# Seven block products for 16 of the 22 contraction tiles of the down product in a decoder trunk's two FFNs

## The chip, the cores and the metric

The kernel runs on one core of a Trainium2 chip. The metric is the device time of one execution in microseconds, the median of several runs.

## The reference

One inference step of a hybrid decoder trunk, for a prompt of 1024 tokens and 8 single tokens of other sequences: 1032 token columns together, width 1024. The part around the change, cut from the reference:

```
x = x + 0.5 * SwiGLU_1(RMSNorm(x))
... one input projection, an RG-LRU and an SSD head group, one output projection ...
x = x + 0.5 * SwiGLU_2(RMSNorm(x))
final RMSNorm

def swiglu(x, w_gate, w_up, w_down):
    return (silu(x @ w_gate) * (x @ w_up)) @ w_down      # (1024 x 2816), (1024 x 2816), (2816 x 1024)
```

All is float32. D_FF is 2816, so the hidden of an FFN has 22 tiles of 128 rows, and the contraction of the down product runs over these 22 tiles.

## The kernel before

Everything is kept transposed: 128 features on the partitions, the 1032 tokens along the free axis. Each float32 operand of TensorE is split into a high and a low part that it can multiply in one pass (type fp32r in the rows), and a product is the sum of three matmuls, high x high, high x low and low x high.

**Gate and up.** Of the 22 pairs of a gate tile and an up tile of an FFN, two are computed plainly. The other 20 are done in 20 groups (`NG`, number q, 0 to 19) by a scheme of seven block products: the outputs of a group are two tiles (two of gate for an even q, two of up for an odd one), cut into 2 x 2 blocks of output tiles by token halves (516 columns, `HT`), the contraction of 8 tiles is cut in two halves of 4, and seven products of blocks and of sums of blocks (p1 to p7, in the order of `ORDER`: p1, p2, p6, p5, p7, p3, p4) replace eight. One product is 4 contraction tiles x 2 pieces of 258 columns x 3 parts = 24 matmuls, a group 168 (L922). Some products accumulate onto others in PSUM, so between two of them another engine must have read or copied the bank: in `group` of TensorE's program (L876) p6 waits for ScalarE's first copy, p7 for the second (`copied`), p3 for the third, which is that of p5, and p4 waits until VectorE has read the bank of p7 (`c22`).

- Weights: SP loads the two raw tiles of a group; VectorE forms four sums of them (`weight_sums`, L1722 to L1728, 128 x 512 each); ScalarE rounds each of the seven operands to its high part (`operand_high`, L1267) and GpSimd forms the low one (`operand`, L693). The ring holds `RING` = 6 operands.
- ScalarE copies p1, p6 and p5 of each group out of PSUM (`part`, L1301) and does the silu of a gate pair in the odd groups (L1334), at the third step of its `group` (L1320). In group 1 of FFN1 it has besides (`extra`) small preparations for later: the table load at L1397 and the operations of `heads` and `lam`.
- VectorE adds the banks to the copies (`corners`, `join`, L1747), reads p4 (`last_corner`, L1767), scales by the norm's factor (`scale`, L1731) and multiplies gate by up (`product`, L1737) into a pair of hidden tiles, which SP stores to DRAM (`store_hidden`, L466).

**Down.** SP loads the hidden tiles back (`load_hidden`, L471), ScalarE rounds them (L1318), VectorE forms the low parts (`hidden_low`, L1779). TensorE multiplies in three blocks of 8, 8 and 6 contraction tiles (`FFN_BLOCKS`); for each block and each of 8 output tiles m, `products` (L805) calls `nine` (L796, L801) for every contraction tile: 3 pieces of 344 columns x 3 parts = 9 matmuls. The weights of such a unit are split by GpSimd (L670, L672) along a plan's list (`make_plan`). VectorE adds 0.5 x the result to x (`residual`, L1820). The last block of FFN2 is done in three pieces of columns for m from 2 on (L1195), so that the final norm can start early; that doesn't change here.

Each engine has its own program in which all waits stand in order; the seam between group 19 and the down product is written out by hand: VectorE's `lows` puts five `hidden_low` among the joins of group 19.

## Time and profile before

| | |
|---|---|
| runs of the kernel before | 2148.04, 2146.0, 2147.6 us; median 2147.6 |
| the profiled execution | 2145.86 us, its span 2144.1 us |
| mean granted clock of TensorE in it | 0.997 of full speed |
| busy share of the span: TensorE, VectorE, ScalarE, GpSimd | 99%, 60%, 36%, 41% |
| chain that ended last, by engine | TensorE 91%, VectorE 4%, ScalarE 2% |
| read from DRAM, written | 149.37 MB, 46.26 MB; 91 GB/s over the span |

The profile is one execution. A span runs from the first to the last instruction that it shows; the execution's own time is 1.8 us more. The chain of waits follows the work that ended last back from the end: where it runs over TensorE's matmuls, nothing else sets the time. A row of the timeline gives the start, the length and the operation, and in brackets the idle time before it with what ended it. A granted clock of 1.00 is TensorE at 2.4 GHz, 0.50 at 1.2 GHz.

### The profile page before, as it was taken

To read this page: it belongs to the slowest core of one execution; us is meant where nothing else is said; L and a number is where in the kernel's file an instruction comes from. 1 tells how busy PE (TensorE), PEld (TensorE's weight loads), DVE (VectorE), ACT (ScalarE), POOL (GpSimd) and SP (SyncE) were. 2 spreads that over 40 slices of the span, in tenths; PEclk is the share of its full clock that TensorE was granted. 3 is DMA by queue.
4 is the path that set the end of the run, shared out by engine and by line. 5 is a ranking of instruction groups with operands and counts; after the bars stand their busy time and mean duration, and the time that the engine had idled before them with its cause. 6 is when DMAs were issued, how large, how long until landed. Compare 5 with 4: busy or idle time off the path is not lost.

```text
span 2144.1 us, 36027 instructions
## 1 busy us (share of the span) xinstructions
PE 2125.4 (99%) x15378; PEld 2094.4 (98%) x15378; DVE 1292.0 (60%) x1157; ACT 782.3 (36%) x1180; POOL 883.9 (41%) x532
## 2 busy tenths in 40 slices
PE   9999999999999999999999999999999999999998
PEld 9999999999999999999999999999999999999998
DVE  7767565562223557878888596786656556542226
ACT  7433333331001224678786540123433333320004
POOL 4544444433433322443444552333544444434440
PEclk9999999999999999999999999999999999999999
DMA  5122121254222422311111422132212212353222
GB/s 170 60 100 73 66 99 68 91 182 145 98 66 84 138 70 89 120 54 50 37 57 62 157 82 90 50 119 72 87 68 92 79 62 97 120 208 99 89 60 80
DMA packets 64752, 197.80 MB, mean 92 GB/s; under 512 B 9416, under 2 KB 18120, under 8 KB 64592
## 3 DMA queue, kind: packets, MB, share of 16 engines
q1 hardware_dynamic: 63440, 194.97, 26.4%
q8 instruction: 122, 2.00, 0.4%
q10 hardware_dynamic: 1152, 0.52, 0.1%
q14 instruction: 38, 0.31, 0.0%
HBM read 149.37 MB, written 46.26 MB: 91 GB/s over the span
## 4 chain that ended last, share of the span: by engine, by line
PE 91%; DVE 4%; ACT 2%; DVEq 1%; issue 1%; POOL 0%; DMA 0%; ACTq 0%; SPq 0%; POOLq 0%
PE banks L801 44%; PE banks L922 36%; PE banks L845 3%; PE banks L1195 2%; DVE h_lo L1779 0%; PE banks L1106 0%; ACT gate_a L1465 0%; PE banks L953 0%; PE banks L960 0%; PE banks L966 0%; PE banks L1084 0%; PE banks L1102 0%; ACT gate_x L1465 0%; PE banks L1076 0%; DVE decay L2083 0%
## 5 line engine op out<-in xcount | busy, mean ns | idle before, releaser
L672 POOL TENSOR_TENSOR w_lo<-w_raw,w_hi 128x1024 fp32r<-128x1024 f32 (+1 forms) x100 | 270.2, 2702 | 170.8 <-DVE xbc L2054 123.2
L670 POOL TENSOR_SCALAR w_hi<-w_raw 128x1024 fp32r<-128x1024 f32 (+1 forms) x91 | 102.1, 1122 | 565.7 <-PE banks L801 510.3
L801 PE MATMUL banks<-h_hi,w_lo 128*128 128x344 f32 x948 | 303.5, 320 | 0.2 <-DVE up L1747 0.2
L801 PE MATMUL banks<-h_lo,w_hi 128*128 128x344 f32 x948 | 302.9, 319 | 0.0
L801 PE MATMUL banks<-h_hi,w_hi 128*128 128x344 f32 x948 | 302.6, 319 | 0.0
L801 PE MATMUL banks<-u_hi,w_lo 128*128 128x344 f32 x864 | 286.2, 331 | 0.4
L801 PE MATMUL banks<-u_hi,w_hi 128*128 128x344 f32 x864 | 276.4, 320 | 0.0
L801 PE MATMUL banks<-u_lo,w_hi 128*128 128x344 f32 x864 | 276.1, 320 | 0.0
L1820 DVE SCALAR_TENSOR_TENSOR x<-banks,x 128x1032 f32<-128x1032 f32 x42 | 51.8, 1233 | 314.8 <-PE banks L801 314.8
L801 PEld LDWEIGHTS banks<-h_hi,w_lo 128*128 128x128 f32 x948 | 178.0, 188 | 0.4 <-DVE up L1747 0.4
L801 PEld LDWEIGHTS banks<-h_hi,w_hi 128*128 128x128 f32 x948 | 178.4, 188 | 0.0
L801 PEld LDWEIGHTS banks<-h_lo,w_hi 128*128 128x128 f32 x948 | 178.2, 188 | 0.0
L801 PEld LDWEIGHTS banks<-u_hi,w_lo 128*128 128x128 f32 x864 | 162.8, 188 | 7.3 <-issue 5.1
L801 PEld LDWEIGHTS banks<-u_hi,w_hi 128*128 128x128 f32 x864 | 162.9, 188 | 5.1 <-issue 4.3
L801 PEld LDWEIGHTS banks<-u_lo,w_hi 128*128 128x128 f32 x864 | 162.9, 189 | 0.0
L922 PE MATMUL banks<-mix_hi,w_lo 128*128 128x258 f32 x864 | 158.1, 282 | 0.0
L922 PE MATMUL banks<-mix_hi,w_hi 128*128 128x258 f32 x864 | 157.9, 282 | 0.0
L922 PE MATMUL banks<-mix_hi,w 128*128 128x258 f32 x832 | 151.7, 283 | 1.7 <-DVE up L1747 1.7
L1747 DVE TENSOR_TENSOR up<-banks,up 128x516 f32<-128x516 f32 x60 | 41.7, 695 | 165.3 <-PE banks L922 162.6
L1318 ACT ACTIVATE h_hi<-stage 128x1032 fp32r<-128x1032 f32 x44 | 45.8, 1065 | 259.7 <-DMA stage<-hidden 226.5
L922 PE MATMUL banks<-x_hi,w 128*128 128x258 f32 x704 | 130.3, 285 | 4.6 <-ACT up L1301 4.6
L922 PEld LDWEIGHTS banks<-mix_hi,w_lo 128*128 128x128 f32 x864 | 134.0, 189 | 0.0
(353 smaller groups left out, 5661.4 us busy)
## 6 DMA issues: line engine op xcount, KB each, us to landing
w_raw<-in_gate_up SPq DMA_DIRECT2D x46, 512.0 KB, 4.4
hidden<-up SPq DMA_DIRECT2D x44, 516.0 KB, 3.6
stage<-hidden SPq DMA_DIRECT2D x44, 516.0 KB, 3.8
raw<-in_gate_up SPq DMA_DIRECT2D x40, 512.0 KB, 4.3
w_raw<-in_w_in SPq DMA_DIRECT2D x36, 512.0 KB, 4.2
w_raw<-in_down SPq DMA_DIRECT2D x32, 512.0 KB, 4.6
x<-in_xt SPq DMA_DIRECT2D x16, 516.0 KB, 6.7
x_kept<-x SPq DMA_DIRECT2D x16, 516.0 KB, 5.1
```

The lines of the kernel that those rows point to most:

```text
L670: pool.tensor_scalar(w_hi[s][:, 0:n], w_raw[s][:, 0:n], 1.0, 0.0, ALU.mult, ALU.add)
L672: pool.tensor_tensor(w_lo[s][:, 0:n], w_raw[s][:, 0:n], w_hi[s][:, 0:n].bitcast(F32), ALU.subtract).then_inc(split, 1)
L801: end = pe.matmul(out[:, c, 0:CH], w[s][:, k * P:(k + 1) * P], x[kx][:, c * CH:(c + 1) * CH], start=(first and n == 0), stop=(last and n = ...
L845: end = pe.matmul(at[:, c, :], w[s][:, k * P:(k + 1) * P], x, start=(k == 0 and n == 0), stop=(k == KT - 1 and n == 2))
L922: end = pe.matmul(out[:, c, :], w[:, part, k * P:(k + 1) * P], x[:, cols], start=(opens and k == 0 and i == 0), stop=(k == 3 and i == 2), ...
L1195: end = pe.matmul(piece_bank(m, here), w[m][:, k * P:(k + 1) * P], x[FFN_BLOCKS[LAST][0] + k][:, here], start=(k == 0 and n == 0), stop=(k ...
L1318: act.activation(f.hh[j][:], f.stage[n][:], ACT.Copy).then_inc(f.hid_hi.sem, 1)
L1747: dve.tensor_tensor(halved(tile), bank, halved(tile), ALU.add).then_inc(f.ev.sem, 1)
L1820: dve.scalar_tensor_tensor(tile, whole(name), 0.5, tile, ALU.mult, ALU.add).then_inc(set_free[s], 1)
```

## The change

Sixteen of the 22 contraction tiles of each down product go through the seven-product scheme too, as 8 further groups (number q, 20 to 27; `NGT` = 28): two blocks of 8 contraction tiles, and in each four groups, one for each pair of output tiles ("side"). Here the weights of the pair take the place of the gate's, and the hidden takes the place of the normed x. Six contraction tiles (`PLAIN`: 0, 1, 18 to 21) stay as they were, 9 matmuls of 344 columns each. The rows of w_down are put in the order of `DOWN_ORDER` ahead of the launch.

- Tokens' side: VectorE forms four sums and differences of each of 8 hidden pairs (`hidden_mixes`, 128 x 516 each, in the even groups 2 to 16 behind the join of p7); SP stores them to DRAM. A block needs seven operands of the hidden ("slots", 128 x 4 x 516, one for each product, shared by its four groups): SP loads them (`load_slot`, rows of 2064 bytes), ScalarE rounds them (`slot_high`), VectorE forms the low parts (`slot_low`). There are 8 slot buffers for 14 slots in an FFN.
- Down groups: 168 matmuls each like the others; VectorE adds 0.5 x each bank straight into two output tiles of x (`down_group`, seven operations of 516 columns), and p6, p7, p3 and p4 wait for its read of p1, p6, p5 and p7.
- ScalarE: in the groups of gate and up the silu, and `extra` with it, now stands one step later, behind the copy of p5.
- VectorE: the seam of group 19 now holds `slot_low` 0 to 2 and the weight sums of group 20, and group 20 `slot_low` 4 to 6.
- PSUM, the plan of units, norms and stores follow suit; the x of the residual is read from other tiles (`x_again`) than before.

```diff
-FFN_BLOCKS = [(0, 8), (8, 8), (16, 6)]
-LAST = len(FFN_BLOCKS) - 1
+BLOCKS, SIDES = 2, 4
+PLAIN = [0, 1, 18, 19, 20, 21]
+N_LAST = len(PLAIN)
+DOWN_ORDER = [2 * (1 + 4 * b + k) + n for b in range(BLOCKS) for n in range(2) for k in range(4)] + PLAIN
...
+ND = BLOCKS * SIDES
+NGT = NG + ND
+NOPS = 7 * NGT
 RING = 6
+SLOTS = 8
+MIXED = 4 * BLOCKS
...
-        for b, (first, n) in enumerate(FFN_BLOCKS):
-            for m in range(KT):
-                p.unit(("d" + tag, b, m), down[m, :, first * P:(first + n) * P], n)
+        for m in range(KT):
+            p.unit(("d" + tag, m), down[m, :, 8 * BLOCKS * P:], N_LAST)
...
+            def down_weights(f, src, q):
+                b, side = divmod(q - NG, SIDES)
+                group_weights(f, q, [src[2 * side + n, :, 8 * b * P:8 * (b + 1) * P] for n in range(2)])
...
+                if 1 <= i <= MIXED:
+                    sp.wait_ge(*f.h_mixed.past(i))
+                    sp.dma_start(d.hidden_mix[:, i - 1], f.part).then_inc(f.mix_stored.sem, 16)
...
+            def load_slot(f, o):
+                b, n = divmod(o, 7)
+                if o == 0:
+                    sp.wait_ge(used, U(("u" + f.tag, 1)) + 1)
+                elif o < SLOTS:
+                    sp.wait_ge(*f.done.past(7 * (NG - 1) + o))
+                else:
+                    sp.wait_ge(*f.done.past(7 * (NG + SIDES - 1) + o - SLOTS + 1))
+                sp.wait_ge(*f.h_stored.past(32 * (4 * (b + 1) + 1)))
+                sp.wait_ge(*f.mix_stored.past(16 * 4 * (b + 1)))
+                two = d.hidden.rearrange("p (i n) t -> p n i t", n=2)
+                here = slice(1 + 4 * b, 5 + 4 * b)
+                mixed = d.hidden_mix[:, 4 * b:4 * b + 4]
+                src = {"p1": two[:, 0, here, 0:HT], "p2": two[:, 1, here, 0:HT], "p6": mixed[:, :, 1, :], "p5": mixed[:, :, 0, :],
+                       "p7": mixed[:, :, 2, :], "p3": two[:, 1, here, HT:T], "p4": mixed[:, :, 3, :]}[ORDER[n]]
+                sp.dma_start(f.slot_raw[o % SLOTS], src).then_inc(f.slot_landed[o % SLOTS].sem, 16)
...
+            def down(f, x_src, src):
+                load_slot(f, 0)
+                for m in range(2):
+                    x_again(f, x_src, m)
+                down_weights(f, src, NG)
+                for m in range(2, 4):
+                    x_again(f, x_src, m)
+                down_weights(f, src, NG + 1)
+                for o in range(1, SLOTS):
+                    load_slot(f, o)
+                down_weights(f, src, NG + 2)
+                store_hidden(f, NG // 2)
+                sp.wait_ge(*f.h_stored.past(32 * (NG // 2 + 1)))
+                for m in range(4, KT):
+                    x_again(f, x_src, m)
+                    down_weights(f, src, q)
+                for o in range(SLOTS, 7 * BLOCKS):
+                    load_slot(f, o)
+                    down_weights(f, src, q)
...
+                    if q >= NG and (q - NG) % SIDES == 0:
+                        pe.wait_ge(*f.slot_split.past(7 * b + n + 1))
...
+                    if q >= NG and name in ("p6", "p7", "p3", "p4"):
+                        pe.wait_ge(*f.ev.past(read_number(q, {"p6": "p1", "p7": "p6", "p3": "p5", "p4": "p7"}[name])))
...
+            def slot_high(f, o):
+                if o == 0:
+                    act.wait_ge(*f.mix_stored.past(16 * MIXED))
+                act.wait_ge(*f.slot_landed[o % SLOTS].past(16 * (o // SLOTS + 1)))
+                act.activation(f.slot_hi[o % SLOTS], f.slot_raw[o % SLOTS], ACT.Copy).then_inc(f.slot_high.sem, 1)
...
+            first_slot, next_slot = 7 * (NG - 1) + 3, 7 * (NG + SIDES - 1) + 3
+            slots_after = {first_slot + n: n for n in range(SLOTS)}
+            slots_after.update({next_slot + o - SLOTS: o for o in range(SLOTS, 7 * BLOCKS)})
 
             def group(f, q, extra=None):
                 for n in range(7):
-                    if n in (0, 2, 3):
+                    o = 7 * q + n
+                    if q < NG and n in (0, 2, 3):
                         part(f, q, ORDER[n])
-                    if 7 * q + n + RING < NOPS:
-                        operand_high(f, 7 * q + n + RING)
-                    if n == 2:
+                    ahead = {7 * NG - RING + n: () for n in (0, 1)}
+                    ahead.update({7 * NG - RING + 2 + n: (7 * NG + n,) for n in range(4)})
+                    ahead[7 * NG - 1] = (7 * NG + 3, 7 * NG + 4, 7 * NG + 5)
+                    if n == 3 and q < NG:
                         if q == 0:
                             first_silu(f)
                         if extra:
...
                             for tile in f.g[(q // 2 + 1) % 2]:
                                 end = act.activation(tile[:], tile[:], ACT.Silu)
                             end.then_inc(f.silu.sem, 1)
+                    for to in ahead.get(o, (o + RING,)):
+                        if to < NOPS:
+                            operand_high(f, to)
+                    if o in slots_after:
+                        slot_high(f, slots_after[o])
...
+            def hidden_mixes(f, i):
+                if i > 1:
+                    dve.wait_ge(*f.mix_stored.past(16 * (i - 1)))
+                b11, b12, b21, b22 = f.u[0][:, 0:HT], f.u[0][:, HT:T], f.u[1][:, 0:HT], f.u[1][:, HT:T]
+                to = [f.part[:, n, :] for n in range(4)]
+                dve.drain()
+                dve.tensor_tensor(to[0], b11, b12, ALU.subtract)
+                dve.tensor_tensor(to[2], b22, b12, ALU.subtract)
+                dve.drain()
+                dve.tensor_tensor(to[1], b22, to[0], ALU.add)
+                dve.drain()
+                dve.tensor_tensor(to[3], b21, to[1], ALU.subtract).then_inc(f.h_mixed.sem, 1)
...
+            def slot_low(f, o):
+                n = o % SLOTS
+                dve.wait_ge(*f.slot_high.past(o + 1))
+                dve.tensor_tensor(f.slot_lo[n], f.slot_raw[n], f.slot_hi[n].bitcast(F32), ALU.subtract).then_inc(f.slot_split.sem, 1)
...
+            def down_group(f, q, between):
+                side = (q - NG) % SIDES
+                even, odd = f.again[2 * side], f.again[2 * side + 1]
+                left, right = slice(0, HT), slice(HT, T)
+                main, second, third = main_bank(q), twos[1], twos[2]
+                if q < NG + SIDES:
+                    for m in (2 * side, 2 * side + 1):
+                        dve.wait_ge(x_landed[m], 32 if f.tag == "1" else 64)
+                for name, bank, x, part in (("p1", main, even, left), ("p2", second, even, left), ("p6", main, even, right),
+                                            ("p5", third, odd, right), ("p7", main, odd, right), ("p3", third, even, right),
+                                            ("p4", main, odd, left)):
+                    dve.wait_ge(*f.done.past(number(q, name) + 1))
+                    dve.drain()
+                    dve.scalar_tensor_tensor(halved(x[:, part]), bank, 0.5, halved(x[:, part]), ALU.mult,
+                                             ALU.add).then_inc(f.ev.sem, 1)
+                    if between.get(name):
+                        between[name]()
...
+                        between = {"p2": lambda: slot_low(f, 0), "p6": lambda: weight_sums(f, NG), "p7": lambda: slot_low(f, 1),
+                                   "p3": lambda: slot_low(f, 2)}
...
+                hooks = {NG: {"p1": lambda: slot_low(f, 4), "p2": lambda: slot_low(f, 5), "p6": lambda: slot_low(f, 6),
+                              "p5": last_pair, "p7": lambda: product(f, NG // 2, 0),
+                              "p3": lambda: (product(f, NG // 2, 1), weight_sums(f, NG + 1))},
+                         NG + 1: {"p7": lambda: slot_low(f, 7)},
+                         NG + SIDES - 1: {"p7": lambda: slot_low(f, 8), "p3": lambda: slot_low(f, 9),
+                                          "p4": lambda: slot_low(f, 10)},
+                         NG + SIDES: {"p1": lambda: slot_low(f, 11), "p6": lambda: slot_low(f, 12), "p5": lambda: slot_low(f, 13),
+                                      "p3": lambda: weight_sums(f, NG + SIDES + 1)},
+                         NGT - 1: {"p3": lambda: hidden_low(f, 0)}}
```

ScalarE in groups 0 and 1 of FFN1. The first row is the copy of p6 of group 1, `up_1<-banks` that of p5. Before:

```order
L1301 ACTIVATE up_0_82<-banks 128x516
L1267 ACTIVATE w_lo<-raw_0_84 128x512
L1397 ACT_TABLE_LOAD
L1397 ACTIVATE heads<-heads 128x16
L1399 ACTIVATE lam<-lam 128x8
L1334 ACT_TABLE_LOAD
L1334 ACTIVATE gate_2_80<-gate_2_80 128x1032
L1334 ACTIVATE gate_3_81<-gate_3_81 128x1032
L1301 ACTIVATE up_1_83<-banks 128x516
```

and with the change:

```order
L1371 ACTIVATE up_0_82<-banks 128x516
L1335 ACTIVATE w_lo<-raw_0_84 128x512
L1371 ACTIVATE up_1_83<-banks 128x516
L1471 ACT_TABLE_LOAD
L1471 ACTIVATE heads<-heads 128x16
L1473 ACTIVATE lam<-lam 128x8
L1403 ACT_TABLE_LOAD
L1403 ACTIVATE gate_2_80<-gate_2_80 128x1032
L1403 ACTIVATE gate_3_81<-gate_3_81 128x1032
```

The copy of p5 has moved ahead of both table loads, `heads`, `lam` and the silu of the first gate pair.

VectorE in group 19 of FFN1, from the join of p2 on. `up_0<-banks` (L1747) are the joins of p2 and p3, `up_1<-banks` with itself the join of p7, the one with `rstd` the read of p4. Before:

```order
L1747 TENSOR_TENSOR up_0_82<-banks,up_0_82 128x516
L1779 TENSOR_TENSOR h_lo_119<-stage_0_91,h_hi_97 128x1032
L1779 TENSOR_TENSOR h_lo_120<-stage_1_92,h_hi_98 128x1032
L1779 TENSOR_TENSOR h_lo_121<-stage_2_93,h_hi_99 128x1032
L1747 TENSOR_TENSOR up_1_83<-banks,up_1_83 128x516
L1779 TENSOR_TENSOR h_lo_122<-stage_3_94,h_hi_100 128x1032
L1747 TENSOR_TENSOR up_0_82<-banks,up_0_82 128x516
L1779 TENSOR_TENSOR h_lo_123<-stage_4_95,h_hi_101 128x1032
```

and with the change, where L1886 are the reads of group 20:

```order
L1821 TENSOR_TENSOR up_0_82<-banks,up_0_82 128x516
L1867 TENSOR_TENSOR slot_lo_107<-slot_raw_115,slot_hi_99 128x4x516
L1796 TENSOR_TENSOR w_sum_1_89<-raw_0_84,raw_1_85 128x512
L1798 SCALAR_TENSOR_TENSOR raw_1_85<-raw_1_85 128x512
L1800 SCALAR_TENSOR_TENSOR w_sum_0_88<-raw_1_85,raw_0_84 128x512
L1802 TENSOR_TENSOR w_sum_2_90<-raw_0_84,w_sum_0_88 128x512
L1821 TENSOR_TENSOR up_1_83<-banks,up_1_83 128x516
L1867 TENSOR_TENSOR slot_lo_108<-slot_raw_116,slot_hi_100 128x4x516
L1821 TENSOR_TENSOR up_0_82<-banks,up_0_82 128x516
L1867 TENSOR_TENSOR slot_lo_109<-slot_raw_117,slot_hi_101 128x4x516
L1841 TENSOR_TENSOR up_1_83<-banks,rstd 128x516
```

`slot_low` of slot 0 and the four weight sums of group 20 (L1796 to L1802) stand between the joins of p2 and p7, and a `slot_low` of 128 x 2064 between any two reads after that.

ScalarE in the same group, with the change. L1371 are the copies of p6 and p5, L1403 the silu, L1377 `slot_high`:

```order
L1335 ACTIVATE w_1_87<-w_raw 128x512
L1371 ACTIVATE up_0_82<-banks 128x516
L1371 ACTIVATE up_1_83<-banks 128x516
L1403 ACTIVATE gate_0_78<-gate_0_78 128x1032
L1403 ACTIVATE gate_1_79<-gate_1_79 128x1032
L1335 ACTIVATE w_hi<-raw_0_84 128x512
L1377 ACTIVATE slot_hi_99<-slot_raw_115 128x4x516
L1335 ACTIVATE w_lo<-raw_0_84 128x512
```

The silu and one operand stand between the copy of p5 and the high part of slot 0; before, the hidden tiles were rounded here (L1318).

## Rows read from the trace of the kernel before

**Rows 1.** The page's head and part 1: busy time, share of the span, instructions.

```profile
span 2144.1 us, 36027 instructions
...
PE 2125.4 (99%) x15378; PEld 2094.4 (98%) x15378; DVE 1292.0 (60%) x1157; ACT 782.3 (36%) x1180; POOL 883.9 (41%) x532
```

**Rows 2.** Chain of waits, its three longest pieces: start us, us, work, instructions.

```profile
97.32 362.13 PE banks L922 x3000
...
469.43 258.16 PE banks L801 x1638
...
1479.02 395.15 PE banks L922 x3288
```

**Rows 3.** TensorE's waits: line, releaser, us in total, times, longest us.

```profile
PE banks L922 <- ACT up L1301: 4.6, 1, 4.6
...
PE banks L922 <- DVE up L1747: 1.7, 2, 0.9
...
PE banks L801 <- DVE up L1747: 0.2, 1, 0.2
```

**Rows 4.** Timeline of ScalarE, groups 0 and 1 of FFN1: start us, us, operation.

```profile
88.08 1.28 ACT L1397 ACT_TABLE_LOAD   x1
...
93.25 0.21 ACT L1399 ACTIVATE lam<-lam 128x8 f32<-128x8 f32 x1 [3.65 <-DVE lam L1823]
...
94.77 2.02 ACT L1334 ACTIVATE gate<-gate 128x1032 f32<-128x1032 f32 x2
96.69 0.58 ACT L1301 ACTIVATE up<-banks 128x516 f32<-128x516 f32 x1
```

**Rows 5.** TensorE by window: length, busy us (instructions), granted clock, DMA share, GB/s.

```profile
98.00:99.00 1.00, 1.00 (x7) 0.50 0.00 0
98.00:108.00 10.00, 10.00 (x74) 0.85 0.01 2
```

**Rows 6.** Timeline of VectorE around groups 18 to 19 of FFN1.

```profile
437.70 1.77 DVE L1722 TENSOR_TENSOR w_sum<-w_raw 128x512 f32<-128x512 f32 x1
439.54 0.69 DVE L1724 SCALAR_TENSOR_TENSOR w_raw<-w_raw 128x512 f32<-128x512 f32 x1
...
445.14 0.70 DVE L1747 TENSOR_TENSOR gate<-banks,gate 128x516 f32<-128x516 f32 x1 [2.17 <-PE banks L922]
445.93 2.22 DVE L1731 TENSOR_TENSOR gate<-gate,rstd 128x1032 f32<-128x1032 f32 x1
...
453.79 0.69 DVE L1747 TENSOR_TENSOR up<-banks,up 128x516 f32<-128x516 f32 x1 [3.27 <-PE banks L922]
...
469.30 1.22 DVE L1779 TENSOR_TENSOR h_lo<-stage,h_hi 128x1032 fp32r<-128x1032 f32 x1
```

**Rows 7.** Timeline of GpSimd in group 18.

```profile
437.62 1.30 POOL L693 TENSOR_TENSOR w_hi<-w_raw,w_hi 128x512 fp32r<-128x512 f32 x1 [2.08 <-ACT w_hi L1267]
```

**Rows 8.** Windows, all engines: busy us of PE, PEld, DVE, ACT, POOL, clock, DMA share, GB/s.

```profile
436.00:446.00 10.00, 10.00 (x86) 10.00 (x85) 7.00 (x9) 3.51 (x6) 4.06 (x4) 1.00 0.59 215
790.00:796.00 6.00, 5.70 (x83) 5.39 (x82) 4.17 (x9) 2.63 (x3) 0.00 (x0) 0.83 1.04 270
1890.00:1892.00 2.00, 2.00 (x15) 2.00 (x14) 1.83 (x3) 0.00 (x0) 0.00 (x0) 1.00 1.04 419
```

**Rows 9.** Timeline of ScalarE in group 19 of FFN1.

```profile
451.39 0.62 ACT L1267 ACTIVATE w<-w_raw 128x512 fp32r<-128x512 f32 x1
...
457.09 2.02 ACT L1334 ACTIVATE gate<-gate 128x1032 f32<-128x1032 f32 x2
459.48 0.60 ACT L1301 ACTIVATE up<-banks 128x516 f32<-128x516 f32 x1 [0.37 <-PE banks L922]
...
468.95 1.06 ACT L1318 ACTIVATE h_hi<-stage 128x1032 fp32r<-128x1032 f32 x1 [2.02 <-DMA stage<-hidden]
```

**Rows 10.** The page's part 5: busy us, mean ns of one.

```profile
L672 POOL TENSOR_TENSOR w_lo<-w_raw,w_hi 128x1024 fp32r<-128x1024 f32 (+1 forms) x100 | 270.2, 2702 | 170.8 <-DVE xbc L2054 123.2
...
L1820 DVE SCALAR_TENSOR_TENSOR x<-banks,x 128x1032 f32<-128x1032 f32 x42 | 51.8, 1233 | 314.8 <-PE banks L801 314.8
```

More of the change, by code:

```diff
@@ L245, in build, with ffn_tiles @@
         f1 = Names()
-        def ffn_tiles(f, tag, x, tt, bb, gate, up, raw, op, sums, stage, late):
+        def ffn_tiles(f, tag, x, again, tt, bb, gate, up, raw, op, sums, late):
             f.tag, f.x = tag, at(f"x{tag}", x, [KT, T])
@@ L1180, in last_sum @@
                         pe.wait_ge(squared["final"], c * KT + KT + n)
-                    pe.matmul(sum_at(n, here), ones[:], (f2.c[(KT - 1) % 2] if end else f2.tot)[:, here], start=not end,
-                              stop=True).then_inc(summed["final"], 1)
+                    pe.matmul(sum_at(n, here), ones[:], (end_c[(KT - 1) % 2] if end else end_tot)[:, here], start=not end,
+                              stop=True).then_inc(norm_summed, 1)
             for c, here in enumerate(PIECES):
@@ L1815, in residual @@
+                for q in range(NG, NGT):
+                    between = dict(hooks.get(q, {}))
+                    if q not in (NG, NG + SIDES, NGT - 1):
+                        between["p2"] = lambda q=q: weight_sums(f, q + 1)
+                    down_group(f, q, between)
+                for t in range(1, N_LAST):
+                    hidden_low(f, t)
+            def residual(f, m):
+                name = ("d" + f.tag, m)
                 s, n = AT[name]
-                if b == 0:
-                    dve.wait_ge(x_landed[m], 32 if f.tag == "1" else 64)
@@ L2272, in tiles, with down @@
         return w.reshape(-1, P, k * P)
+    def down(w):
+        order = [n * P + r for n in DOWN_ORDER for r in range(P)]
+        return tiles(np.asarray(w)[order])
     def gate_up(gate, up):
@@ L2316 @@
         "gate_up2": gate_up(ffn2_w_gate[0], ffn2_w_up[0]),
[L2317 removed]
+        "down2": down(ffn2_w_down[0]),
     }
```

410 lines of the change are left out of this document (199 added, 211 removed).

## The prediction

> **What bounds the kernel now.** I read the page's totals first. TensorE is busy for 99% of a span of 2144.1 us, VectorE 60%, ScalarE 36%, GpSimd 41% [rows 1]. So a microsecond of matmuls taken away is a microsecond gained, unless another engine comes late, and only stretches in which the others are dense can make that happen. Second, the chain of waits: its three longest pieces are the matmuls of the seven-product groups (3000 and 3288 of them) and of FFN1's down product (1638) [rows 2]. They give the price of one matmul: 258.16/1638 = 0.1576 us for 344 columns, 362.13/3000 = 0.1207 and 395.15/3288 = 0.1202 us for 258 columns; I take 0.1203. Third, TensorE's waits: nearly everything is in three entries, 4.6 us once on ScalarE at L1301 and 1.7 + 0.2 us on VectorE at L1747 [rows 3]. The other engines hide for now, so the whole case turns on the new seam between gate and up and the down product, where ScalarE and VectorE must turn 14 slots per FFN into high and low parts.
>
> All sums stand against the profiled execution, 2145.86 us; the median of the three runs is 1.7 us above it, and differences from change to no change can be told here from about 0.2% (4 us).
>
> **Fewer columns.** An FFN loses 16 tiles x 8 outputs x 9 = 1152 matmuls of 344 columns and gains 8 x 168 = 1344 of 258. That is 1152 x 0.1576 = 181.6 us against 1344 x 0.1203 = 161.7 us: -19.9 us per FFN, **-39.7 us** for both. All of it lies on the path, since TensorE is the bound. A block's seven products of 24 matmuls take 2.89 us each, a group 20.2 us.
>
> **Old stalls that go.** At the old seam VectorE does five `hidden_low` around the joins of group 19, and p4 waits for the join of p7: the 1.7 + 0.2 us of [rows 3]. In the new order that work is replaced by other work, costed below: **-1.9 us**.
>
> The 4.6 us are in group 1 of FFN1. ScalarE has a table load at 88.08, waits 3.65 us for `lam`, loads another table, does two silus of 2.02 us together, and only then, at 96.69, copies p5 out of PSUM (`part`, L1301) [rows 4]. That copy is what p3 waits for. Right after the stall TensorE's granted clock is 0.50, its lower level of 1.2 GHz, and the ten us from 98 hold 74 matmuls at a mean of 0.85 [rows 5], where the full clock gives 83 (10/0.1203): 9 matmuls, 1.1 us, and with some records missing up to 1.7. I take 1.5. The change puts the copy of p5 ahead of table, `lam` and silu, at about 90: 4.63 + 1.5 = **-6.1 us**. What is late next: operands behind the silu, whose ring is six products deep (17 us), so nothing.
>
> **Hidden mixes.** Four more VectorE operations of 516 columns for each of 8 pairs, in the even groups behind the join of p7. By the row of such a join, 0.70 us, and the 0.69 us of 512 columns, they cost 3.1 us with drains [rows 6]. In group 18 VectorE joins at 445.14, scales for 2.22 us, and the next join at 453.79 had 3.27 us of idle time before it [rows 6]. 3.1 fits in 3.27, and what doesn't fit has the slack of the group after. Cost 0; without that cover about 0.8 us per pair with a GpSimd turn in it, 6 us per FFN. The stores (2 MB per FFN more) share queues that moved 215 GB/s at a share of 0.59 [rows 8].
>
> **The new seam.** By the spacing of products, group 19 begins at 447.7, its p5 ends at 459.3 (its copy starts at 459.48 [rows 9]) and p4 would start at 465.05. p4 of group 19 waits for VectorE's join of p7. In the new order VectorE has `slot_low(0)` and the weight sums of group 20 ahead of that join, and `slot_low(0)` waits for `slot_high(0)`, which ScalarE does behind the copy of p5 and the silu. Durations: silus 2.02 and copy 0.60 from their rows [rows 9]. `slot_high` is an activation copy of 4 x 516 = 2064 columns: 0.62 at 512 and 1.06 at 1032 [rows 9] extend to 1.93. `slot_low`: 0.69 at 512 and 1.22 at 1032 [rows 6] extend to 2.29. The chain: 459.5 + 0.6 copy + 2.0 silu + 0.55 one operand + 1.93 + 2.29 + 2.85 (four weight sums of 0.69 with gaps) + 0.76 (join) = 470.5. TensorE waits **5.5 us**.
>
> From there VectorE is the bound until p4 of group 20: six `slot_low` 13.7 us, seven reads of PSUM at 0.76, 5.3, the last scales 2.0, together 21.0, so 491.5. TensorE alone needs 2.9 + 17.4 and would be there at 490.9. To the 21.0 comes the turn of GpSimd. The row of a weight sum at 437.70 shows 1.77 us where the next ones take 0.69, and GpSimd's operand operation runs over 437.62 to 438.92 [rows 6, 7]; the joins that read PSUM stay at 0.69 and 0.70. So an operation of VectorE with two SBUF inputs that meets one of GpSimd waits for it: up to 1.08 us here. There are about six such meetings in the stretch (an operand of 1.3 us per product), 0.53 us each beyond what gaps absorb: 3.2 us, so 494.7, or **3.8 us** late. The Trainium skill's page "SBUF — State Buffer", section "SBUF: two separate sides", says that the port pair of the two is an exclusive lock for a whole instruction, and the other "fully blocks". By that rule each meeting costs up to a whole operand operation, and the row of 1.77 us agrees; without it the stretch would cost 0.6 instead of 3.8.
>
> Then come the lower clock after a stall of 5.5 us (1.1 to 1.7, as after group 1; I take 1.5), sums of group 21 that come late (0.9), and at group 24, where six `slot_low` with their reads take 3.05 us each against products of 2.89, 1.0 plus one meeting: 1.2. At the end of group 27, the plain products wait for `hidden_low(0)` (1.22 us) and for the weights, which GpSimd splits at 2.70 us a unit [rows 10]: between 0.9 and 2.6, taken as 2.0. Per FFN 5.5 + 3.8 + 1.5 + 0.9 + 1.2 + 2.0 = 14.9: **+29.8 us**. Bounds per FFN: nothing (the slots keep pace), and 24 (each of 14 `slot_low` meets GpSimd for a full 1.3, on top 7 us).
>
> Reads of down groups go straight into x (0.76 by the joins; the eviction of 1032 columns that they replace took 1.23 [rows 10]), spread evenly: 0. ScalarE and GpSimd have 64% and 59% free: 0. The program's start and end keep their order: 0.
>
> **Sum**: -39.7 - 1.9 - 6.1 + 29.8 = -17.9, so 2145.9 - 17.9 = **2128 us**.
>
> **The rivals.**
> A: VectorE is not held up by GpSimd, or meets it seldom. Then the seam costs 5.5 + 0.6 + 1.5 + 1.0 + 1.1, near 10 per FFN: 2145.9 - 47.7 + 20 = 2118. For it: joins are never held. Against it: the 1.77 us.
> B: no seam stall at all (ScalarE reaches slot 0 early enough and VectorE waits nowhere): 2145.9 - 47.7 = 2098. Against it: the order has the silu ahead of `slot_high(0)`.
> C: the slot operations cost more than a straight line through two points says, since their 4 pieces of 516 are one operation with a longer access pattern. At 2.7 and 2.2 us: six more 0.4 in the seam, in group 24 again, with 0.3 for ScalarE, 5.7 per FFN: 2139. At 3.0 and 2.5 us it would be 2150, slower by 4.
> D, the other side: the slots' transfers. Every block of four groups needs 7 loads of 128 x 4 x 516 x 4 bytes = 1.06 MB. Those of the second block can start only when products of group 23 have ended, and 6 of them, 6.36 MB, must land in some 27.5 us: 231 GB/s. The first block's 7.4 MB have some 36 us: 206 GB/s. At full share the trace shows 270 GB/s for the state tensors' 512-byte rows and 419 for longer ones, and 215 at a share of 0.59 beside the groups' weights [rows 8]. At 190 GB/s the waits are 9 us per FFN and eat the gain: that is the point from which it decides. At 150 GB/s they are 42.4 - 27.5 + 49.3 - 36 = 28 per FFN: 2128 + 56 = 2184, slower. For it: weights and stores of the same groups use the queues too. Against it: every row at full share is above 231.
> E: the silus' move in group 1 gains nothing, because ScalarE has still to wait for something else there: 2128 + 6 = 2134.
>
> **How the numbers follow.** My forecast's case (seam 12 to 17 per FFN: 2122 to 2133) has 0.52, A 0.20, B 0.05, C 0.10 (of it 0.04 above 2145), D 0.06, E 0.07. Faster by over 0.2% is everything but the ends of C and D: 0.91; within 0.2% 0.03; slower 0.06. The range goes from 2112, below A, to 2142, above E and the first form of C; B, D and the far end of C stay outside.
>
> **What would show it.** Right: two stretches of TensorE idle of 4 to 7 us in p4 of group 19 of each FFN, put down to the join of p7 on VectorE; a granted clock of 0.50 after them; `slot_low` at about 2.3 us, some at 3 to 3.5 beside GpSimd; a gain at the first group of 6 us by 108; down groups of 20.2 us away from the seam. Wrong: TensorE waiting for DMA at the slots (D), `slot_high` or `slot_low` above 2.6 everywhere (C), no seam stall (B), or VectorE stalls in groups 21 to 23 or 25 to 27, for which I have no term. Then the sum is off by what the waits of TensorE add up to, since the columns' 39.7 us rest on the spacing of nearly 8,000 matmuls and hardly move.

## The result and the profile after

The change makes the kernel slower by a hair: 2150.5 us median of 15 runs (2147.8 to 2153.9) against 2147.1 of 15 runs of the kernel before, a ratio of 1.0017 with a 95% interval of 1.0009 to 1.0024. The forecast was 2128 with a range of 2112 to 2142: it was wrong. The spread of the change goes with the granted clock: 2147.8 to 2149.2 us in runs with a mean of 0.993, 2153.2 to 2153.9 in those with 0.989 or 0.990. The profiled execution took 2150.97 us; its page begins:

```profile
span 2149.2 us, 37492 instructions
...
PE 2099.4 (98%) x15762; PEld 2064.2 (96%) x15762; DVE 1488.9 (69%) x1361; ACT 868.2 (40%) x1288; POOL 950.5 (44%) x580
```

TensorE does 384 matmuls more than in [rows 1] but is busy for 26 us less. That is less than the 39.7 of the columns mostly because matmuls at half clock count as busy for twice as long; the columns' saving is priced from e8 further down. VectorE went from 1292 to 1489 us. The chain of waits has these long pieces of matmuls, against [rows 2]:

```profile
58.09 395.22 PE banks L993 x3288
...
465.15 4.63 PE banks L993 x24
...
509.94 16.01 PE banks L993 x120
...
1475.10 395.15 PE banks L993 x3288
...
1927.05 17.21 PE banks L993 x120
...
2087.39 22.26 PE banks L1263 x126
```

They give a balance by stretches. The groups of gate and up of FFN1 go from 58.09 to 453.31, 395.2 us, where the kernel before needed 57.83 to 459.45, 401.6: **6.4 us gained**. From the end of that piece to the first matmul of the input projection (725.11 after, 727.58 before) it is 271.8 against 268.1 us: **3.7 lost**. From the end of FFN2's gate and up (1475.10 + 395.15, and [rows 2]) to the last block in pieces (2087.39 after, 2082.31 before) it is 217.1 against 208.1: **9.0 lost**. Between the FFNs 1.5 us are gained, which e10 below shows too though it touches nothing there, and the first group starts 0.3 later. Together that is the +5.1 us between the spans. Of the columns 19.9 us per FFN were to come, and 0.95 from the old stall; with these two taken as forecast, the new seam and the down groups cost 24.5 us in FFN1 and 29.9 in FFN2, where 14.9 were forecast: 54.4 us given back for some 48 gained. TensorE's waits, against [rows 3]:

```profile
PE banks L993 <- DVE up L1821: 12.1, 2, 6.1
PE banks L993 <- DVE x_pair L1886: 8.8, 5, 4.9
PE banks L993 <- DVE x_again L1886: 8.7, 5, 4.8
PE banks L863 <- DVE h_lo L1871: 4.6, 5, 1.1
PE banks L993 <- DVE slot_lo L1867: 3.8, 2, 2.0
```

All five are waits for VectorE: the join of p7 at the seams, the reads of down groups (`x_again` in FFN1, `x_pair` in FFN2), low parts. None is for a DMA. The row on ScalarE's copy from [rows 3] is gone. Where they lie, in the timeline of TensorE in FFN1:

```profile
465.15 0.80 PE L993 MATMUL banks<-mix_hi,w 128*128 128x258 f32 x2 [6.08 <-DVE up L1821]
...
477.37 0.47 PE L993 MATMUL banks<-slot_hi,w 128*128 128x258 f32 x2 [1.83 <-DVE slot_lo L1867]
...
509.94 0.80 PE L993 MATMUL banks<-slot_hi,w_lo 128*128 128x258 f32 x2 [4.84 <-DVE x_again L1886]
...
595.96 0.50 PE L993 MATMUL banks<-slot_hi,w 128*128 128x258 f32 x2 [1.99 <-DVE x_again L1886]
```

The first is the forecast stall before p4 of group 19, 6.08 us. The second is in group 20. The third is 4.84 us before p7 of group 21, the fourth 1.99 in group 25. These two, and three more of 0.6 us before p7 of groups 22, 23 and 26, are behind weight sums; group 24 has none. VectorE there:

```profile
499.39 0.70 DVE L1886 SCALAR_TENSOR_TENSOR x_again<-banks,x_again 128x516 f32<-128x516 f32 x1 [1.60 <-PE banks L993]
503.30 1.67 DVE L1796 TENSOR_TENSOR w_sum<-raw,raw 128x512 f32<-128x512 f32 x1 [3.21 <-POOL w_hi L757]
505.04 1.60 DVE L1798 SCALAR_TENSOR_TENSOR raw<-raw 128x512 f32<-128x512 f32 x1
...
508.40 0.69 DVE L1802 TENSOR_TENSOR w_sum<-raw,w_sum 128x512 f32<-128x512 f32 x1
509.19 1.48 DVE L1886 SCALAR_TENSOR_TENSOR x_again<-banks,x_again 128x516 f32<-128x516 f32 x2
...
527.39 1.62 DVE L1798 SCALAR_TENSOR_TENSOR w_raw<-w_raw 128x512 f32<-128x512 f32 x1
```

In group 21 VectorE reads p2 at 499.39, is idle for 3.21 us until GpSimd has made the last operand that its weight sums wait for, and then needs 5.8 us for four sums, three of which take 1.60 to 1.67 instead of 0.69. Only then, at 509.19, does it read p6, for which p7 waits. In group 22 two of the four meet GpSimd (at 527.39 and at 529.85, 1.62 us each). GpSimd in the same stretch:

```profile
503.11 1.31 POOL L757 TENSOR_TENSOR w_lo<-w_raw,w_lo 128x512 fp32r<-128x512 f32 x1
...
515.13 3.43 POOL L757 TENSOR_TENSOR w_lo<-raw,w_lo 128x512 fp32r<-128x512 f32 x1 [3.96 <-ACT w_lo L1335]
```

It makes one operand behind the other here (the row is the last of four without a gap, from 499.36 on); they are those of group 21, whose own sums VectorE had made only at 493.23 to 496.2. The last row stands beside the low part of slot 7. And the granted clock behind three of the waits, the last in FFN2 (columns as in [rows 5]):

```profile
465.00:467.00 2.00, 1.85 (x8) 0.50 1.05 391
510.00:512.00 2.00, 2.00 (x9) 0.50 0.03 8
1926.00:1932.00 6.00, 4.95 (x23) 0.50 0.01 2
```

### The profile page after: what moved, and what is told of

Same layout as the page of the kernel before. It is cut to its first block, busy times and chain, and to the rows that moved or that the text cites. A ratio compares the mean times of both kernels' runs of the same rounds, so it can differ in the third digit from the quotient of the medians.

```text
span 2149.2 us, 37492 instructions
## 1 busy us (share of the span) xinstructions
PE 2099.4 (98%) x15762; PEld 2064.2 (96%) x15762; DVE 1488.9 (69%) x1361; ACT 868.2 (40%) x1288; POOL 950.5 (44%) x580
## 4 chain that ended last, share of the span: by engine, by line
PE 84%; DVE 8%; ACT 3%; DVEq 2%; issue 1%; POOL 1%; DMA 0%; ACTq 0%; SPq 0%; POOLq 0%
PE banks L993 47%; PE banks L863 26%; PE banks L907 3%; PE banks L1263 2%; DVEq L1797 1%; DVE w_sum L1802 1%; ACT slot_hi L1377 1%; DVE w_sum L1800 1%; DVE h_lo L1871 1%; DVE slot_lo L1867 1%; DVE raw L1798 1%; DVE w_raw L1798 0%; PE banks L1174 0%; ACT gate_a L1539 0%; DVE w_sum L1796 0%
## 5 line engine op out<-in xcount | busy, mean ns | idle before, releaser
L736 POOL TENSOR_TENSOR w_lo<-w_raw,w_hi 128x1024 fp32r<-128x1024 f32 (+1 forms) x68 | 166.9, 2454 | 166.4 <-DVE xbc L2182 123.6
L734 POOL TENSOR_SCALAR w_hi<-w_raw 128x1024 fp32r<-128x1024 f32 (+1 forms) x59 | 67.0, 1135 | 345.8 <-PE banks L863 276.6
L993 PEld LDWEIGHTS banks<-mix_hi,w 128*128 128x128 f32 x832 | 130.9, 192 | 12.6 <-DVE up L1821 12.5
L993 PEld LDWEIGHTS banks<-mix_hi,w_hi 128*128 128x128 f32 x864 | 133.7, 189 | 0.0
L757 POOL TENSOR_TENSOR w_lo<-w_sum,w_lo 128x512 fp32r<-128x512 f32 x58 | 78.8, 1358 | 119.6 <-ACT w_lo L1335 119.6
L757 POOL TENSOR_TENSOR w<-w_sum,w 128x512 fp32r<-128x512 f32 x54 | 83.8, 1554 | 106.0 <-ACT w L1335 105.8
L993 PE MATMUL banks<-slot_hi,w_lo 128*128 128x258 f32 x608 | 115.1, 289 | 11.1 <-DVE x_pair L1886 5.6
L993 PE MATMUL banks<-mix_lo,w_lo 128*128 128x258 f32 x432 | 122.5, 284 | 0.0
L993 PE MATMUL banks<-mix_lo,w_hi 128*128 128x258 f32 x432 | 122.3, 283 | 0.0
L993 PE MATMUL banks<-mix_lo,w 128*128 128x258 f32 x416 | 118.8, 286 | 0.0
```

The lines of the kernel that those rows point to most:

```text
L734: pool.tensor_scalar(w_hi[s][:, 0:n], w_raw[s][:, 0:n], 1.0, 0.0, ALU.mult, ALU.add)
L736: pool.tensor_tensor(w_lo[s][:, 0:n], w_raw[s][:, 0:n], w_hi[s][:, 0:n].bitcast(F32), ALU.subtract).then_inc(split, 1)
L757: pool.tensor_tensor(to[:, 1, :], src, to[:, 0, :].bitcast(F32), ALU.subtract).then_inc(f.op_ready.sem, 1)
L993: end = pe.matmul(out[:, c, :], w[:, part, k * P:(k + 1) * P], x[:, cols], start=(opens and k == 0 and i == 0), stop=(k == 3 and i == 2), ...
```

## The experiments

**e1_copy_first: the moved silu on the kernel before.** ScalarE's `group`:

```diff
-                    if 7 * q + n + RING < NOPS:
-                        operand_high(f, 7 * q + n + RING)
-                    if n == 2:
+                    if n == 3:
...
+                    if 7 * q + n + RING < NOPS:
+                        operand_high(f, 7 * q + n + RING)
```

> The kernel before with one part of the change alone: ScalarE's silu, and what stands with it, goes one step later in every group, behind the copy of p5. Theory 1 (the move ends the stall in group 1 of FFN1 and does nothing else): TensorE's 4.6 us on ScalarE at the copy are gone and the half-clock stretch after them too, so 6.1 us less than before, about 2141. Theory 2 (the trace of the change gains its 6.4 us in the groups for another reason, such as the new order of loads): the stall stays, within 1 us of before.

Measured: 2150.0 us, ratio 1.0013 (1.0004 to 1.0022), slower than before. Both theories missed the total. The chain's piece of gate and up and the waits:

```profile
58.25 395.21 PE banks L922 x3288
...
2085.17 22.26 PE banks L1195 x126
```

```profile
PE banks L922 <- DVE up L1747: 8.9, 2, 4.5
```

The 6.4 us in group 1 are gained (395.2 us, as in the change), so the term was right. But at the old seams the high parts of the hidden tiles stand behind the silu too, and VectorE's low parts and the join of p7 behind them: two waits of 4.5 us for 0.9. In FFN2 the way from gate and up to the last block is 214.1 us (1871.07 to 2085.17) for 208.1. The 395.2 us also price the hidden mixes: this kernel has none, the change has 8 sets of them in each FFN, and the stretch takes the same time to 0.01 us (in FFN2 too, 395.15 in both). They cost nothing, as forecast.

**e10_group1: the same in group 1 of FFN1 alone.**

```diff
+                    late = f.tag == "1" and q == 1
-                    if n == 2:
+                    if n == (3 if late else 2):
```

(with the operand of that step behind it)

> The kernel before with the silu and what stands with it behind the copy of p5 in group 1 of FFN1 alone, all other groups as they were. Theory 1 (the move in all groups gained its 6 us in group 1 and gave 9 back at the two seams, where the high parts of the hidden tiles stand behind the silu): 6.1 us less than before, 2141, and the waits for the join of p7 at the seam are 0.9 us each again. Theory 2 (the stall only goes elsewhere): within 2 us of before.

Measured: 2140.6 us, ratio 0.9970 (0.9959 to 0.9981), 6.7 under before; the seams' waits are as in [rows 3]:

```profile
PE banks L922 <- DVE up L1750: 1.7, 2, 0.9
PE banks L922 <- ACT gate L1301: 1.7, 1, 1.7
```

Theory 1 holds: the 4.6 us on `up` are gone. The total is a less exact check than it looks, though. The second row is a wait in group 0, ahead of the edited group, that no other profiled execution has; with a low clock behind it (0.60 in 74:78) the stretch of gate and up takes 398.7 us here (57.1 to 455.8), 3.5 more than in e1, and 1.5 us of this execution's gain lie between the FFNs. Where the stall of group 0 comes from is open. This one line of the change, put where it helps, makes the kernel faster, which the change as a whole does not.

**e5_slot0_early: slot 0's high part ahead of the silu.**

```diff
-            slots_after = {first_slot + n: n for n in range(SLOTS)}
+            slots_after = {first_slot + n: n for n in range(1, SLOTS)}
+            slots_after[7 * (NG - 1)] = 0
```

> The change with the high part of slot 0 made by ScalarE behind the first product of group 19 instead of behind the silu. Theory 1 (the chain copy of p5, silu, high part, low part, weight sums, join of p7 makes the 6.1 us at the seam, and VectorE's work without a gap carries them on to group 21): the stall before p4 of group 19 is gone, the slots up to group 20 end 4 to 6 us earlier, and the stall in group 21 starts from there: 5 us less per FFN and some of the half clock, 2137. Theory 2 (the slots' landing, some 11 us after the issue of slots 1 to 3, sets the pace behind it): the 6.1 us go, but most of them come back by p4 of group 20: 0 to 2 us per FFN, 2147 to 2150.

Measured: 2133.4 us, ratio 0.9945 (0.9931 to 0.9958), 17.0 under the change, more than theory 1 said. Waits:

```profile
PE banks L993 <- DVE x_again L1887: 8.9, 5, 5.0
...
PE banks L993 <- issue: 3.2, 6, 0.8
PE banks L993 <- DVE slot_lo L1868: 2.0, 2, 1.0
```

The two waits of 6.1 us have gone and nothing has taken their place: VectorE joins p7 at once, and what was left of the way through group 20 is 1.0 us and three waits of 0.2 to 0.8 with it. TensorE's waits are 10.3 us shorter in all. The rest is the clock: this kernel has a mean of 0.996, the change 0.991. It falls only behind the waits in group 21 here, where the two pieces of 120 matmuls take 16.62 and 16.55 us for 14.4: 4.3 us, where the same count gives 12.6 in the change (see the part on the lower clock). The waits in groups 21 to 26 stand untouched at 9 us per FFN, so they did not come from the seam's lateness.

**e2_sums_later: the weight sums of the down groups behind the read of p3.**

```diff
-                    if q not in (NG, NG + SIDES, NGT - 1):
-                        between["p2"] = lambda q=q: weight_sums(f, q + 1)
+                    if q == NG + SIDES - 1:
+                        between["p2"] = lambda q=q: weight_sums(f, q + 1)
+                    elif q not in (NG, NG + SIDES, NGT - 1):
+                        between["p3"] = lambda q=q: weight_sums(f, q + 1)
```

> The change with VectorE's weight sums in groups 21, 22, 25 and 26 moved from behind the read of p2 to behind the read of p3. Theory 1 (behind p2 they start while GpSimd makes operands, each sum that meets one takes 1.6 us for 0.7, and the reads that p7 waits for stand behind them): TensorE's waits for the reads of the down groups fall from 8.7 us to about 1.3 per FFN, and with the half clock after them the whole is 20 us under the change, about 2130. The sums then take 0.7 each. Theory 2 (the sums are slow wherever they stand, or the operands come late by themselves): they stay at 1.6, and the waits move to the operands of p6, at most 5 us gained, 2145 or more.

Measured: 2131.3 us, ratio 0.9931 (0.9919 to 0.9944), 19.2 under the change, as theory 1 said. Of ten waits for reads two are left, one in group 23 of each FFN, whose sums stayed behind p2:

```profile
PE banks L993 <- DVE x_again L1886: 2.0, 1, 2.0
```

and the sums where GpSimd is idle take 0.7 us each:

```profile
574.13 0.68 DVE L1796 TENSOR_TENSOR w_sum<-w_raw 128x512 f32<-128x512 f32 x1
```

The move does two things at once: it takes the sums out of the way of the read that p7 waits for, and it puts them where GpSimd is idle. e2 does not tell them apart; e6 shows that the second alone is enough.

**e6_pool_narrow: GpSimd hardly works in the down groups.**

```diff
-                pool.tensor_tensor(to[:, 1, :], src, to[:, 0, :].bitcast(F32), ALU.subtract)
+                c = slice(0, 16 if q >= NG else 512)
+                pool.tensor_tensor(to[:, 1, c], src[:, c], to[:, 0, c].bitcast(F32), ALU.subtract)
```

> The change with GpSimd's low part of the operands in the eight down groups made in 16 of 512 columns only; the other columns keep what was there, so a part of the low weights of the down product is left out. VectorE then hardly ever meets GpSimd there. Theory 1 (VectorE's operations with two inputs from SBUF wait for GpSimd's): the weight sums take 0.7 us each instead of 1.6, the low parts of the slots 2.3 instead of up to 3.15, TensorE's waits in the groups 20 to 27 fall by more than half, 15 to 25 us less than the change in all, 2126 to 2136. Theory 2 (the sums of down weights are slow for another reason): they stay at 1.6 and the time within 6 us of the change.

Measured: 2119.9 us, ratio 0.9874 (0.9861 to 0.9888), 30.6 under the change. The groups of VectorE between 500 and 600 us, first of the change, then of this kernel:

```profile
L1867 DVE TENSOR_TENSOR slot_lo<-slot_raw,slot_hi 128x2064 fp32r<-128x2064 f32 x7 | 17.6, 2513 | 0.0
L1798 DVE SCALAR_TENSOR_TENSOR raw<-raw 128x512 f32<-128x512 f32 x3 | 4.8, 1616 | 0.2
```

```profile
L1868 DVE TENSOR_TENSOR slot_lo<-slot_raw,slot_hi 128x2064 fp32r<-128x2064 f32 x7 | 16.1, 2298 | 0.0
...
L1799 DVE SCALAR_TENSOR_TENSOR raw<-raw 128x512 f32<-128x512 f32 x2 | 1.4, 692 | 0.2
```

The mean of the same sum falls from 1616 to 692 ns, those of the slots' low parts from 2513 to 2298: theory 1's mechanism is shown. All ten waits for reads are gone; the largest left is the seam's, 5.0 us for 6.1:

```profile
PE banks L994 <- DVE up L1822: 10.0, 2, 5.0
```

The gain is above its 15 to 25 us. The kernel also drops GpSimd's own time, for which VectorE waited 3.21 us in group 21 and waits 0.73 here, and with the waits the half clock behind them; how the 30.6 us divide was not measured.

**e3_warm19 and e4_warm21: matmuls into the waits.** In `group` of TensorE's program, ahead of the wait named (here e4's; e3 has group 19, p4 and 40):

```diff
+                    if q == NG + 1 and name == "p7":
+                        pe.wait_ge(*f.op_ready.past(o + 1))
+                        pe.wait_ge(*f.ev.past(second_read(q)))
+                        for i in range(32):
+                            k, c = i // 6 % 4, i % 2
+                            hi, lo = tokens[name](k)
+                            pe.matmul(twos[1][:, c, :], f.op[op_slot(o)][:, 0, k * P:(k + 1) * P],
+                                      hi[:, c * QT:(c + 1) * QT], start=True, stop=True)
```

> The change with 40 more matmuls of 258 columns (copies of those of p4, into a bank that nobody reads then) ahead of the wait of p4 of group 19, where TensorE is idle for 6.1 us. They keep it busy for 4.8 of these. Theory 1 (what the seam costs behind this stall is set by VectorE, which works without a gap until group 21): p4 runs at the full clock, but its end waits for nothing that counts; the wait in group 20 grows by as much, and the time stays within 2 us of the change, 2149 to 2151. Theory 2 (the half clock after a stall adds to the path everywhere): 2 us per FFN less, 2146.

> The change with 32 such matmuls ahead of the wait of p7 of group 21 for the read of p6 (4.8 and 4.9 us idle, followed by about 3 us at half clock in FFN1 and 6.5 in FFN2). Theory 1 (the half clock is what follows the idle engine, and from here on TensorE sets the pace): the granted clock stays at 1.00 behind the wait, and half of the two stretches is gained, 4 to 5 us in all, 2146. Theory 2 (the clock falls for another reason, or the matmuls hinder VectorE's sums): no gain, 2150 or more.

Measured: e3 2146.5 us (ratio 0.9997, 0.9987 to 1.0006), e4 2147.4 (1.0002, 0.9993 to 1.0011), 4.0 and 3.1 under the change. The clock behind the filled waits, e3's in group 19, then e4's in group 21 of FFN1 and FFN2:

```profile
465.00:469.00 4.00, 4.00 (x34) 1.00 0.98 361
```

```profile
512.00:514.00 2.00, 2.00 (x19) 1.00 0.00 0
1928.00:1930.00 2.00, 1.79 (x15) 1.00 0.00 0
598.00:600.00 2.00, 2.00 (x11) 0.50 0.00 0
```

It stays at 1.00, where the change shows 0.50 at 465:467, 510:512 and 1926:1932. Of e4's 3.1 us the noise is a larger part than of e3's 4.0, since the intervals of its ratio and the change's overlap. Its theory 1 holds in the clock, with less gained than the 4 to 5 us: in its profiled execution, in FFN1, the clock fell behind the next wait, of 2.0 us in group 25 (598:600), where the change's execution had kept it. For e3 my theory 1 fell: p4 at half clock was on the path, since in the change ScalarE makes slot 3 and VectorE reads p4 only when p4 is done, and VectorE then stands idle for 2.11 us (the second row):

```profile
470.54 0.68 DVE L1841 TENSOR_TENSOR up<-banks,rstd 128x516 f32<-128x516 f32 x1
473.33 3.15 DVE L1867 TENSOR_TENSOR slot_lo<-slot_raw,slot_hi 128x2064 fp32r<-128x2064 f32 x1 [2.11 <-ACT slot_hi L1377]
```

So VectorE did not work without a gap there. Theory 2 said 2 us per FFN, which is the 4.0.

**e7_both: both mends.** The edits of e5 and e2, with the sums of group 24 behind the read of p6 of group 23.

```diff
+                    if q == NG + SIDES - 1:
+                        between["p6"] = lambda q=q: weight_sums(f, q + 1)
```

> The change with both mends: slot 0's high part behind the first product of group 19, and the weight sums of the down groups behind the read of p3 (those of group 24 behind the read of p6). Theory 1 (the two cost independently of each other: the seam and its way through group 20, and the sums' place): their gains add, 17.0 + 19.2 us under the change, and a little for the sums of group 24: 2112 to 2115. Theory 2 (VectorE is full up to group 21, so that what the one gives back the other takes): at most the larger gain and some more, 2125 to 2130.

Measured: 2110.9 us, ratio 0.9829 (0.9816 to 0.9843), 39.5 under the change for 17.0 + 19.2 one by one. They add, with 3.3 us more; in group 23 the two waits of 2.0 us that e2 had left are gone. The waits that are left:

```profile
PE banks L863 <- DVE h_lo L1872: 4.6, 5, 1.1
PE banks L993 <- issue: 3.2, 6, 0.8
PE banks L993 <- DVE slot_lo L1868: 2.3, 2, 1.3
```

**e9_both_narrow: the edit of e6 on e7.**

> The kernel with both mends, and GpSimd's low part of the operands in the eight down groups made in 16 of 512 columns only (the rest of these low weights is left out). Theory 1 (once the weight sums stand where GpSimd is idle, its turns cost only the 0.3 us that each low part of a slot loses): 1 to 3 us less, 2108 to 2110. Theory 2 (GpSimd's turns are still most of what the seam costs): 6 us or more, 2105 or less.

Measured: 2106.9 us, ratio 0.9812 (0.9798 to 0.9825), 4.0 under e7, between the two theories. The same removal was worth 30.6 us on the change. What the change paid for GpSimd was the place of the sums, far more than the turns as such. What the turns still cost e7 is in group 20: its low parts take 2.6 us there, in this kernel 2.3, and of e7's 5.5 us of waits 2.0 are left:

```profile
PE banks L994 <- DVE slot_lo L1869: 2.0, 2, 1.0
```

**e8_seam: what else VectorE's and ScalarE's order gives.** On e7:

```diff
-                              "p5": last_pair, "p7": lambda: product(f, NG // 2, 0),
-                              "p3": lambda: (product(f, NG // 2, 1), weight_sums(f, NG + 1))},
-                         NG + 1: {"p7": lambda: slot_low(f, 7)},
+                              "p7": lambda: weight_sums(f, NG + 1), "p4": last_pair},
+                         NG + 1: {"p1": lambda: product(f, NG // 2, 0), "p2": lambda: product(f, NG // 2, 1),
+                                  "p7": lambda: slot_low(f, 7)},
...
-                         NGT - 1: {"p3": lambda: hidden_low(f, 0)}}
+                         NGT - 1: {"p7": lambda: hidden_low(f, 0), "p3": lambda: (hidden_low(f, 1), hidden_low(f, 2))}}
...
-                for t in range(1, N_LAST):
+                for t in range(3, N_LAST):
```

and in ScalarE's `group`, for group 19 alone, the silu back at the third step, ahead of the copy of p5.

> The kernel with both mends and three more moves: in group 19 the silu goes ahead of the copy of p5 again; in group 20 VectorE's last scales and products go behind the read of p4 and into group 21, with the weight sums of group 21 behind the read of p7; at the end the low parts of the first three plain tiles go among the reads of group 27. Theory 1 (what is left of TensorE's waits, 4.6 us at the plain tiles and 5.5 in groups 20, is VectorE's order): the 4.6 us go and half of the 5.5: 7 us under the kernel with both mends, 2104. Theory 2 (in groups 19 and 20 VectorE is simply full, 2.3 to 2.8 us of low part and 0.7 of a read in each 2.9): the 4.6 go, the 5.5 stay: 2106 or 2107.

Measured: 2105.3 us, ratio 0.9803 (0.9789 to 0.9816), the fastest kernel of the study, 42 us under before. Its waits:

```profile
PE banks L993 <- DVE slot_lo L1870: 3.4, 2, 2.1
...
PE banks L993 <- issue: 1.6, 4, 0.6
```

The 4.6 us at the plain tiles are gone; of the 5.5 in group 20 5.0 stay. By the waits that is theory 2; the median lies between the numbers of the two. VectorE is full there with a low part and a read per product, and this order gives no more. That it is full is in part GpSimd's doing: e9, with the old order, has 2.0 us of waits there.

## Why the prediction was wrong, step by step

**Fewer columns, -39.7: right**, as far as the parts can be told apart. With VectorE's waits almost gone (e8) the kernel is 42 us under before; -39.7 - 1.9 - 6.1 make -47.7, and e8 still has 5 us of waits at slots. The price of a matmul can be read too. In FFN1 of e8 one unbroken piece holds 1224 matmuls of the down groups, 0.1204 us each, where I had 0.1203:

```profile
478.77 147.33 PE banks L993 x1224
```

**The stall of group 1, -6.1: right**, 6.4 in the balance and 6.4 in e1's stretch; that e10's total is 6.7 is in part luck. The sentence beside it, that nothing is late next, was wrong: I followed the move only in the group in which it helps. It stands in all groups, and in group 19 it lengthens a chain (e1: 4.5 us for 0.9). In the change the same move stands in the forecast stall of 5.5 as "2.0 silu", where I took it as given.

**Hidden mixes, 0: right** (395.2 us with and without).

**The stall at p4 of group 19, +5.5 per FFN: right**, 6.08 and 6.05. Its chain held link by link: the silu at 453.84, slot 0's high part 1.92 us at 456.27 and low part 2.31 at 458.21, where I had 1.93 and 2.29 from straight lines through [rows 6, 9], then sums and join. The sums took 3.97 us where I had 2.85, since the first was held for 1.06; that more than makes up the 0.6 us by which the stall is longer:

```profile
458.21 2.31 DVE L1867 TENSOR_TENSOR slot_lo<-slot_raw,slot_hi 128x2064 fp32r<-128x2064 f32 x1 [9.52 <-ACT slot_hi L1377]
460.44 1.75 DVE L1796 TENSOR_TENSOR w_sum<-raw,raw 128x512 f32<-128x512 f32 x1
...
464.41 0.69 DVE L1821 TENSOR_TENSOR up<-banks,up 128x516 f32<-128x516 f32 x1
```

**On to p4 of group 20, +3.8: less**, 1.83. Of seven low parts four lost 0.3 to 0.85 us to GpSimd, 1.9 us in all where I had 3.2; GpSimd yields too (3.43 us for an operand beside slot 7, in its row above).

**The step that failed** is "sums of group 21 that come late (0.9)" and "at group 24 ... 1.2", 2.1 us together. Group 24 has no wait at all. The groups 21 to 23, 25 and 26 measured 4.84 + 1.99 and, with three of 0.57 to 0.64, 8.7 us in FFN1, and 8.8 in FFN2. I had costed the weight sums of the first group only, at the seam, and looked at the later down groups for their PSUM reads and low parts. Yet the row of [rows 6] that I used for the slots, 1.77 us for a sum beside GpSimd, belongs to a weight sum. Each further down group has four of them between the reads of p2 and p6, on which p7 hangs. From p2's end to p7's start there are two products, 5.8 us; a read, four sums with two of them held, and a read of p6 need 0.7 + 4.9 + 0.7 = 6.3. The 0.6 us could have been worked out ahead. The 4.84 comes out of the same sum once it is known that in group 21 three sums are held and 3.2 us of waiting for the operands come first, but that only the trace of the change showed. e2 shows that the place of the sums was the cause, e6 that it was so because of GpSimd.

**The lower clock, +1.5 per FFN: far too small.** It fell behind three waits in FFN1 and four in FFN2, and in FFN2 stayed at 0.50 throughout 1926:1932; I had priced one stretch per FFN, from the one row that [rows 5] gave. The pieces of the chain behind these waits give its price. 24 matmuls took 4.63 us behind the first wait and 4.39 behind the second, for 2.89 at 0.1203 each, and 120 took 16.01 behind the third, for 14.4: 4.8 us in FFN1. In FFN2 the pieces of 4.47, 4.63, 17.21 and 16.19 us give 7.8 in the same way. e3 and e4 took 4.0 and 3.1 us off by filling one wait in each FFN.

Together: of the 54.4 us given back 38.0 are waits (18.3 and 19.7), 12.6 the clock, and 3.8 are left, of the order of 0.2 us at each restart of TensorE (120 matmuls took 14.69 us behind a wait of 0.64, for 14.4). The forecast's 29.8 had 26.8 of waits and 3.0 of clock. So the later groups' sums (17.5 for 4.2) are the largest part of the miss and the clock (12.6 for 3.0) the second; even my bound of 24 per FFN was passed in both.

**The end seam, +2.0: right**, 1.7 and 2.9; e8 removed it.

Of the rivals, D (DMA) did not occur: no wait of TensorE is for a transfer, and the sixteen slots that come from the mixes, 1 MB each, landed in a median of 7.7 us (the page's part on DMA issues; the last column):

```profile
slot_raw<-hidden_mix SPq DMA_DIRECT2D x16, 1032.0 KB, 7.7
```

C did not either (1.92 and 2.30 us for the slot operations away from GpSimd), nor B, nor E (the 6.4 us came). A (2118) came out of e6, where GpSimd is out of the way, at 2120. The range missed since no case held the down groups' own sums; the prediction itself said that it had no term for stalls in groups 21 to 23 or 25 to 27, and that is where they were.

## What to carry to other kernels

Cost a repeated stage by its steady period, operation by operation on the engine that joins it, before costing its seam: here 0.6 us per group showed as a plain sum of rows, and one late set of sums as 4.8. When two engines hold each other up, move the short operations to where the other is idle and where no wait hangs on them; that was worth 19 us here, and with both mends in place removing most of the other engine's work gave only 4 more. A move made "in every iteration" should be followed to the last iteration, where other work is queued behind it.

## What the hardware showed that I had not expected

- An operation of VectorE with two inputs from SBUF took 1.60 to 1.67 us for 0.69 when it fell in with GpSimd's operand, and up to three of four in a row were held. That the drains between the sums are what lets GpSimd in is inferred from the times; no run took the drains away. The reads of PSUM, with one input from SBUF, were not held: 0.68 us at 470.54, beside an operand of GpSimd from 470.51 on. Against a low part of 2.3 us GpSimd pays more, up to 3.4 us for 1.3, and VectorE 0.3 to 0.85. The Trainium skill, page "SBUF — State Buffer", section "SBUF: two separate sides", lets whichever of the two starts first keep the shared ports for a whole instruction. The trace agrees: from 450 to 560 us no operation lost more than one of the other engine's takes (VectorE at most 1.06 us of 1.3, GpSimd at most 2.1 of 2.3).
- The lower clock did not follow from the wait's length alone: behind 2.0 us it fell in one execution (e4, 598:600) and not in another of the same place (the change, where 596:602 is at 1.00), while in FFN2 of the change it fell there too, behind 1.98 us. Behind the waits of 4.8 and 4.9 us in group 21 it stayed at 0.50 for 3 us in FFN1 and nearly 6 in FFN2. 32 matmuls in the wait kept it at 1.00 (e4).
